# Two token tiles per weight unit in three products, and three small moves in a two-block transformer kernel

## The chip, the cores and the metric

The kernel runs on one core of one Trainium2 chip. Its time is the device time of one execution, in microseconds; the time given for a kernel is the median of its runs. The engines are TensorE (PE, with its weight loads shown apart as PEld), VectorE (DVE), ScalarE (ACT), GpSimd (POOL) and SyncE (SP, which here only starts transfers). Each runs its own program in order, and they meet through semaphores.

## The reference

Two transformer blocks on 512 tokens of width 1024, in float32, the second one also on 256 context tokens.

```python
# first block
h = rmsnorm(x, g_pre); proj = h @ w_in         # split into qa ka va gate_a qi ki wi qb kb vb fb gate_b
att_a = dsa_branch(...)                        # top-k chosen keys, softmax
att_b = fox_branch(...)                        # causal attention with a decay
y_a = (att_a * silu(gate_a)) @ w_branch_a;  y_b = (att_b * silu(gate_b)) @ w_branch_b
m_a, m_b = split(sigmoid(h @ w_merge))
out = (m_a * y_a + m_b * y_b) @ w_out          # chunks wo0, wo1
x = x + rmsnorm(out, g_post)                   # x1
e = p @ w_ple                                  # chunks ple0, ple1
gate = sigmoid(x @ w_ple_gate)                 # chunks pg0, pg1
x = x + rmsnorm(gate * e, g_ple)               # x2
# second block, layer 0 (even) and layer 1 (odd)
hx = rms_norm(x, norm_pre) * (1 + sc_x) + sh_x; px = hx @ w_in   # the same for the context
mx = even_mixer(...)   # differential attention (two score maps) over context and own keys, short convolution
x = x + g_x * rms_norm(mx @ w_out, norm_post)  # chunks eo0, eo1; the result is x3
mx = odd_mixer(...)    # neighbourhood attention, Fourier mixing
x = x + g_x * rms_norm(mx @ w_out, norm_post)  # chunks oo0, oo1
```

## The kernel before

Every large product is made in three passes: each float32 operand is split into a rounded high part and the rest, its low part, and high·high, high·low and low·high are added up in PSUM. The weights come as one stream of **granules** of 1 MB, each of four **units** (128 rows by 512 columns), into the two halves of a buffer `RAW` (L1415, SP). For each unit ACT copies the high part to its place (`high`, L1439), and POOL subtracts it from the raw weights for the low part (`low_weights`, L1258). SP loads a granule once the one before the last has been split. PE waits for both parts of a unit (`w_hi`, `w_lo`). Most units go round a ring of four places (`ROOM`); for some chunks spare places are free, so that eight or more units can lie ready: the first four of wo1 and of oo1, all of eo1.

A product of 512 tokens is either computed **unit by unit** (`gemm`: for each unit, all four token tiles of 128, in four PSUM banks) or **tile by tile** (`by_tiles`, L784 to L812, and the loop at L1234 to L1244 for oo1): all eight units for the first token tile, then all eight for the second, and so on. The first tile waits for each unit as it is made; the other three find them there. Tile by tile, a tile's result is complete before the next begins, and the engines behind it can start on it. The order of PE's program is written out by hand; the other engines' programs follow it by hand too.

**Around wo1.** PE runs wo0 (unit by unit), wo1 (L967, tile by tile), ple0 and ple1. For each tile t of wo1 DVE copies the result out of PSUM (L2436), multiplies by g_post (L2132), inverts the root (L2138) and adds to x (L2143), in this order and tile after tile. ACT squares and sums the tile after DVE's copy (`norm_tile`, L1476), then takes the root (L1478). ACT makes the high weights of ple0 after the root of tile 2 (L1726), and those of ple1 after tile 3; POOL makes the low ones behind that.

**Around x2.** pg1 is computed tile by tile. For each tile t ACT runs one step of a loop (L1765 to L1773):

```python
gate_out(4 + t)                    # sigmoid of pg1's tile t, from PSUM
if t: x2_squared(t - 1)            # waits for DVE's x2, then square (L1476) and root (L1478)
high(UNITS["e_q"][min(3 * t + 1, 7)] if t < 3 else UNITS["e_k"][3])
act.wait_ge(sig("ge"), 5 + t)      # DVE has multiplied the gate and e
norm_tile("e", t, M_E[t], 4)       # square and root of e
```

Sigmoid and square root need different function tables on ACT; a load of one is an ACT_TABLE_LOAD in the trace. It stands where the program first needs the other function. Square and copy need no load in either state. After the last step ACT squares x2's tile 3; DVE normalises (L2489), and PE turns the normalised tiles (L819), which it needs before e_q of the 512 tokens. Meanwhile PE computes e_q and e_k for the context from the weights that ACT's loop makes.

**The even attention** has 48 steps: per pair of heads four short ones (context queries, scores 128 by 256) and eight wide ones (128 by 768). `score_even` (L1032) puts the two score maps of a step m = 0, 1 at bank 2m; a wide map takes that bank and the next (`open_two`). DVE takes the maxima (L2550), ACT the exponentials (L1829), which free the banks; between the scores PE works on slices of other products.

**Around eo1.** eo0 (unit by unit), eo1 (L1129, tile by tile, after tile 0 the turning of a modulation row, L757), then both for the context, then the turning of x3 (L819). Per tile, ACT copies the result (L1930), stores x3 of the tile before and squares it, squares this tile, and DVE weighs, inverts and adds; then the next tile. ACT makes n_q's weights after the last tile's squares. x3n, written by DVE at L2647, is what the turning waits for.

**Around oo1**, the last product: ACT squares each tile from PSUM (L2097), DVE multiplies and adds to x3, SP and ACT store it.

**The start.** SP loads x in four transfers, then granules 0 and 1, then constants. ACT squares and roots the four tiles of x, makes unit 0's high part, and takes x turned by PE out of PSUM; DVE makes its low part (L2177). `keys` is the first product.

## Time and profile before

| | us |
|---|---|
| median of 3 runs (lowest, highest) | 1278.9 (1278.81, 1279.24) |
| the profiled execution, and its span from first to last instruction | 1282.1, 1280.3 |
| PE busy in the span | 1235.3 (96%) |
| DVE busy | 673.2 (53%) |
| ACT busy | 632.9 (49%) |
| POOL busy | 461.6 (36%) |

All times in the text are counted from the start of the span. Matmuls are pipelined: the record of a 512-column matmul is 0.39 us long, but the next one starts 0.23 us after it, so "busy" for PE covers small losses, and an idle time in brackets counts only from the end of the record before. `[1.62 <-POOL w_low L1258]` behind an instruction says that the engine was idle for 1.62 us ahead of it and that POOL's instruction of line 1258 released it. In rows by windows, PEclk is the TensorE clock granted, as a share of 2.4 GHz: 0.50 is 1.2 GHz.

### The profile page before, as it was taken

The page shows a single profiled execution, that of the slowest core. Times are in us where ns is not written, and L with a number is a line of the kernel's source. Part 1 is how long each engine was busy: PE and PEld are TensorE (multiplying, and loading weights), DVE is VectorE, ACT ScalarE, POOL GpSimd, SP SyncE. Part 2 cuts the span into 40 slices and gives each one's busy share as a digit, 9 for nine tenths or more (in the row PEclk, how much of TensorE's full clock was granted, in tenths as well). Part 3 has the DMA queues.
Part 4 walks back from the last instruction along what each step waited for, and adds up shares of the span by engine and source line. Part 5 has one row for each costly group of instructions (what it writes and reads, how often), then busy time and mean ns, then how long its engine had stood idle before and what let it go on. Part 6 is the DMA issues. An engine that isn't in the chain of part 4 may idle for free. (4 is left out here: it accounts for less than half of the span.)

```text
span 1280.3 us, 19570 instructions
## 1 busy us (share of the span) xinstructions
PE 1235.3 (96%) x7148; PEld 990.4 (77%) x7148; DVE 673.2 (53%) x1294; ACT 632.9 (49%) x1354; POOL 461.6 (36%) x360
## 2 busy tenths in 40 slices
PE   7999999999999999899999999999999999999997
PEld 5877777776788788788878888787878788777785
DVE  4576965755314254647475765723815600655453
ACT  6544327655533356723366666626345422645433
POOL 5544343321344535612332333332343123322351
PEclk9999999999999999999999999999999999999999
DMA  6332541111322613230434322211254221222542
GB/s 234 117 98 70 194 165 66 45 47 36 133 94 94 225 72 132 75 140 25 153 113 190 130 83 100 100 67 52 89 215 145 90 103 66 100 67 67 175 134 87
DMA packets 28429, 140.33 MB, mean 110 GB/s; under 512 B 4304, under 2 KB 5712, under 8 KB 15728
## 3 DMA queue, kind: packets, MB, share of 16 engines
q1 hardware_dynamic: 21584, 117.72, 26.0%
q10 hardware_dynamic: 6752, 21.35, 5.0%
q8 instruction: 60, 0.98, 0.3%
q14 instruction: 33, 0.27, 0.1%
HBM read 122.74 MB, written 6.29 MB: 101 GB/s over the span
## 5 line engine op out<-in xcount | busy, mean ns | idle before, releaser
L1258 POOL TENSOR_TENSOR w_low<-w_raw,w_high 128x512 fp32r<-128x512 f32 x256 | 348.7, 1375 | 641.7 <-ACT w_high L1439 641.1
L1439 ACT CAST w_high<-w_raw 128x512 fp32r<-128x512 f32 x256 | 153.8, 622 | 259.3 <-PE psum L663 170.6
L663 PE MATMUL psum<-x_high,w_high 128*128 128x512 f32 x528 | 219.2, 415 | 4.6 <-DVE x_low L2177 1.0
L663 PE MATMUL psum<-x_high,w_low 128*128 128x512 f32 x528 | 206.6, 391 | 0.0
L663 PE MATMUL psum<-x_low,w_high 128*128 128x512 f32 x528 | 206.2, 391 | 0.0
L663 PEld LDWEIGHTS psum<-x_high,w_high 128*128 128x128 f32 x528 | 99.6, 189 | 34.1 <-issue 10.1
L663 PEld LDWEIGHTS psum<-x_high,w_low 128*128 128x128 f32 x528 | 99.1, 188 | 21.6
L663 PEld LDWEIGHTS psum<-x_low,w_high 128*128 128x128 f32 x528 | 99.6, 189 | 16.6 <-issue 1.0
L663 PE MATMUL psum<-w_high,x_high 128*128 128x512 f32 x224 | 88.3, 394 | 0.8 <-POOL w_low L1258 0.6
L2550 DVE TENSOR_REDUCE small<-psum 128x1 f32<-128x768 f32 (+1 forms) x96 | 70.0, 771 | 35.3 <-PE psum L1043 35.3
L663 PE MATMUL psum<-w_high,x_low 128*128 128x512 f32 x224 | 87.3, 390 | 0.0
L663 PE MATMUL psum<-w_low,x_high 128*128 128x512 f32 x224 | 87.2, 389 | 0.0
L1287 POOL TENSOR_SCALAR arena<-arena,small 128x768 f32<-128x768 f32 (+1 forms) x48 | 40.5, 844 | 96.6 <-DVE small L2557 96.6
L1829 ACT ACTIVATE arena<-psum,small 128x768 f32<-128x768 f32 (+1 forms) x84 | 63.3, 760 | 14.3 <-DVE small L2550 13.9
L1838 ACT COPY arena<-psum 128x512 f32<-128x512 f32 (+1 forms) x80 | 36.7, 459 | 66.5 <-PE psum L1051 66.1
L663 PEld LDWEIGHTS psum<-w_high,x_high 128*128 128x128 f32 x224 | 42.0, 188 | 14.2 <-issue 4.5
L663 PEld LDWEIGHTS psum<-w_high,x_low 128*128 128x128 f32 x224 | 42.1, 188 | 8.9
L663 PEld LDWEIGHTS psum<-w_low,x_high 128*128 128x128 f32 x224 | 42.1, 188 | 8.4
L691 PE MATMUL psum<-x_high,w_high 128*128 128x512 f32 x96 | 42.1, 438 | 0.5 <-DVE arena L2543 0.5
L2562 DVE SCALAR_TENSOR_TENSOR arena<-arena,small 128x768 f32<-128x768 f32 (+1 forms) x36 | 30.1, 835 | 19.5 <-POOL arena L1287 19.5
L691 PE MATMUL psum<-x_high,w_low 128*128 128x512 f32 x96 | 37.8, 394 | 0.0
L691 PE MATMUL psum<-x_low,w_high 128*128 128x512 f32 x96 | 37.6, 392 | 0.0
(484 smaller groups left out, 2807.0 us busy)
## 6 DMA issues: line engine op xcount, KB each, us to landing
w_raw<-stream SPq DMA_DIRECT2D x98, 1024.0 KB, 4.9
x_kept<-arena ACTq DMA_DIRECT2D x8, 512.0 KB, 4.6
arena<-x_kept ACTq DMA_DIRECT2D x8, 512.0 KB, 5.6
arena<-bias ACTq DMA_DIRECT2D x8, 512.0 KB, 4.5
q_masked<-e_q_high SPq DMA_DIRECT2D x24, 96.0 KB, 2.5
arena<-x SPq DMA_DIRECT2D x4, 512.0 KB, 5.2
arena<-x ACTq DMA_DIRECT2D x4, 512.0 KB, 5.1
arena<-ctx ACTq DMA_DIRECT2D x4, 512.0 KB, 4.5
```

The lines of the kernel that those rows point to most:

```text
L663: mm = pe.matmul(o, l, r, start=(first and n == 0 and kind != "fc"), stop=(last and n == len(passes) - 1))
L691: mm = pe.matmul(o, l, r, start=k == 0 and n == 0, stop=k == NK - 1 and n == 2)
L1258: pool.tensor_tensor(PLACE[u][1], RAW[:, g % 2, u % 4, :], PLACE[u][0].bitcast(F32), ALU.subtract).then_inc(w_lo, 1)
L1287: pool.tensor_scalar(second, second, SM[:, RINV + c + 1:RINV + c + 2], SM[:, 82:83], ALU.mult, ALU.mult)\
L1439: act.copy(PLACE[u][0], RAW[:, g % 2, u % 4, :]).then_inc(w_hi, 1)
L1829: frees(act.activation(map_place(s, m), PS[:, 512 * b:512 * b + w], ACT.Exp, bias=scr(NEGMAX + c), accum_out=scr(ROWSUM + c)), key)
L1838: frees(act.copy(E_PT[:, 2 * (d % 2) + hh, P * c:P * c + w], ps[:, 0:w]), key)
L2550: dve.tensor_reduce(scr(NEGMAX + 2 * (s % 4) + m), PS[:, 512 * b:512 * b + w], AX.X, ALU.max, negate=True).then_inc(sig("e_neg"), 1)
L2562: dve.scalar_tensor_tensor(e0, e0, scr(RINV + c), e1, ALU.mult, ALU.add).then_inc(sig("e_p"), 1)
```

## The change

1. `by_tiles` gets a parameter `together`: the first `together` token tiles are computed side by side, unit by unit, in as many banks, and the rest tile by tile. wo1 and eo1 use `together=2`. oo1's own loop is replaced by `by_tiles` with `together=2`; its last tile now takes the units in the order 4 to 7, 0 to 3, as the other chunks did.
2. In ACT's loop round x2, a square root of a single column stands right after each sigmoid.
3. In the even attention, short steps use banks 2m and 2m + 1 in turn.
4. Granule 0 comes in two transfers: unit 0 alone, with its own semaphore (`stored`, which counts 16 more at the end for it), and units 1 to 3.

```diff
--- before.py
+++ after.py
@@ -781,35 +781,37 @@
                 if chunk in GUEST and GUEST[chunk][1] < 4:
                     due.append(GUEST[chunk])
 
-            def by_tiles(chunk, x, after=None, gives_back=True):
+            def by_tiles(chunk, x, after=None, gives_back=True, together=1):
 
                 units = UNITS[chunk]
-                for t in range(ST):
-                    rows = slice(P * t, P * t + P)
-                    acc = next_bank((chunk, t))
-                    ks = [*range(4, NK), *range(4)] if t == ST - 1 else range(NK)
+                for first in [0, *range(together, ST)]:
+                    group = range(together) if first == 0 else (first,)
+                    accs = {t: next_bank((chunk, t)) for t in group}
+                    ks = [*range(4, NK), *range(4)] if ST - 1 in group else range(NK)
                     for k in ks:
                         u = units[k]
-                        if t == 0:
+                        if first == 0:
                             pe.wait_ge(w_hi, u + 1)
                             pe.wait_ge(w_lo, u + 1)
                             unit_read.add(u)
                         (hi, lo), (wh, wl) = x[k], PLACE[u]
-                        for n, (l, w) in enumerate(((hi, wh), (hi, wl), (lo, wh))):
-                            mm = pe.matmul(acc[:, :], l[:, rows], w, start=k == ks[0] and n == 0,
-                                           stop=k == ks[-1] and n == 2)
-                        if k == ks[-1]:
-                            fills_bank(mm, (chunk, t))
-                            bk, n = fills[chunk, t]
-                            done = (bank_full[bk], n + 1)
-                        elif t == ST - 1 and gives_back:
-                            used[0] += 1
-                            mm.then_inc(w_used, 1)
-                            done = (w_used, used[0])
-                        if t == ST - 1 and gives_back:
-                            unit_done[u] = done
+                        for t in group:
+                            rows = slice(P * t, P * t + P)
+                            for n, (l, w) in enumerate(((hi, wh), (hi, wl), (lo, wh))):
+                                mm = pe.matmul(accs[t][:, :], l[:, rows], w, start=k == ks[0] and n == 0,
+                                               stop=k == ks[-1] and n == 2)
+                            if k == ks[-1]:
+                                fills_bank(mm, (chunk, t))
+                                bk, n = fills[chunk, t]
+                                done = (bank_full[bk], n + 1)
+                            elif t == ST - 1 and gives_back:
+                                used[0] += 1
+                                mm.then_inc(w_used, 1)
+                                done = (w_used, used[0])
+                            if t == ST - 1 and gives_back:
+                                unit_done[u] = done
                     if after:
-                        after(t)
+                        after(first)
 
             def turns(name, tiles, src, ks):
 
@@ -964,7 +966,7 @@
             gemm("wo0", X, ready=split("mrg_lo"))
 
 
-            by_tiles("wo1", X)
+            by_tiles("wo1", X, together=2)
             gemm("ple0", B, ready=turned("pT"))
             gemm("ple1", B)
 
@@ -1036,7 +1038,7 @@
                     pe.wait_ge(sig(f"{kind}_stacked{hh}"), 96 * (pr + 1))
                 for m in range(2):
                     key = ("e", "S", s, m)
-                    acc = (open_two if x else open_bank)(key, 2 * m)
+                    acc = open_two(key, 2 * m) if x else open_bank(key, 2 * m + s % 2)
                     q, k = stack("q", head, m)[0:96, c:c + P], stack("k", head, m)[0:96]
                     for c0 in range(0, w, 512):
                         c1 = min(c0 + 512, w)
@@ -1126,7 +1128,7 @@
             pool[0] = (3, 7, 4, 5, 6)
             gemm("eo0", mixed, mixed_c, ready=lambda k: pe.wait_ge(sig("mix_lo"), 3 * (k // 2) + 3), part="x")
             pool[0] = (0, 1, 2, 6, 4)
-            by_tiles("eo1", mixed, lambda t: turn_due(), gives_back=False)
+            by_tiles("eo1", mixed, lambda t: turn_due(), gives_back=False, together=2)
             pool[0] = (3, 7)
             for k in range(NK):
                 unit("eo0", k, mixed, mixed_c, "c")
@@ -1231,17 +1233,7 @@
                            ("fmix", j))
             mixed = [(KH[:, k, 0:S], KL[:, k, 0:S]) for k in range(4)] + X[4:]
             gemm("oo0", mixed, ready=split("nix_lo"))
-            for t in range(ST):
-                rows = slice(P * t, P * t + P)
-                acc = next_bank(("oo1", t))
-                for k, u in enumerate(UNITS["oo1"]):
-                    if t == 0:
-                        pe.wait_ge(w_hi, u + 1)
-                        pe.wait_ge(w_lo, u + 1)
-                    (hi, lo), (wh, wl) = mixed[k], PLACE[u]
-                    for n, (l, w) in enumerate(((hi, wh), (hi, wl), (lo, wh))):
-                        mm = pe.matmul(acc[:, :], l[:, rows], w, start=k == 0 and n == 0, stop=k == NK - 1 and n == 2)
-                fills_bank(mm, ("oo1", t))
+            by_tiles("oo1", mixed, gives_back=False, together=2)
 
 
         SSQ, NEGMAX, ROWSUM, RINV, TOP8 = 0, 16, 24, 32, 40
@@ -1252,7 +1244,9 @@
             def low_weights(first, last):
                 for u in range(first, last + 1):
                     g = granule_of(u)
-                    if u % 4 == 0:
+                    if u == 0:
+                        pool.wait_ge(sig("stored"), 16)
+                    elif u % 4 == 0 or u == 1:
                         pool.wait_ge(raw_in[g % 2], 16 * (g // 2 + 1))
                     pool.wait_ge(w_hi, u + 1)
                     pool.tensor_tensor(PLACE[u][1], RAW[:, g % 2, u % 4, :],
@@ -1412,6 +1406,11 @@
                         filled(sp, ("mod%d_%d" % mod, 0))
                     else:
                         sp.wait_ge(sig("mod_half"), MODS.index(mod) + 1)
+                if g == 0:
+                    sp.dma_start(RAW[:, 0, 0, :], dram["stream"][0][:, 0:512]).then_inc(sig("stored"), 16)
+                    sp.dma_start(RAW[:, 0, 1:4, :].rearrange("p a n -> p (a n)"),
+                                 dram["stream"][0][:, 512:]).then_inc(raw_in[0], 16)
+                    continue
                 sp.dma_start(RAW[:, g % 2, :, :].rearrange("p a n -> p (a n)"),
                              dram["stream"][g]).then_inc(raw_in[g % 2], 16)
             for t in range(ST):
@@ -1432,7 +1431,9 @@
                 while at[0] <= min(upto, N_UNITS - 1):
                     u = at[0]
                     g = granule_of(u)
-                    if u % 4 == 0:
+                    if u == 0:
+                        act.wait_ge(sig("stored"), 16)
+                    elif u % 4 == 0 or u == 1:
                         act.wait_ge(raw_in[g % 2], 16 * (g // 2 + 1))
                     if before_in_place[u] is not None:
                         act.wait_ge(*unit_done[before_in_place[u]])
@@ -1766,6 +1767,7 @@
                 if t == 3:
                     high(UNITS["e_k"][0])
                 gate_out(4 + t)
+                act.activation(scr(95), scr(95), ACT.Sqrt)
                 if t:
                     x2_squared(t - 1)
                 high(UNITS["e_q"][min(3 * t + 1, 7)] if t < 3 else UNITS["e_k"][3])
@@ -2099,7 +2101,7 @@
                 act.activation(scr(8 + t), scr(8 + t), ACT.Sqrt, bias=scr(SSQ + t), scale=1.0 / D).then_inc(sig("out_root"), 1)
             act.wait_ge(sig("x4"), 2 * ST)
             act.dma_start(columns_of(out, ST - 1)[:, :, 512:], N_O[:, ST - 1, 512:]).then_inc(sig("stored"), 16)
-            act.wait_ge(sig("stored"), 2 * 16 * ST)
+            act.wait_ge(sig("stored"), 16 + 2 * 16 * ST)
 
 
         @block.vector
```

## Rows read from the trace of the kernel before

**Rows 1.** The granted clock over the whole span.

```profile
core 0: 1280.3 us, clock 0.995
```

**Rows 2.** PE's waits: waiting line, releaser; us in total, times, longest us.

```profile
PE psum L1043 <- ACT arena L1829: 2.9, 2, 1.5
...
PE psum L799 <- POOL w_low L1258: 2.5, 4, 1.6
PE psum L651 <- POOL w_low L1258: 2.5, 2, 2.1
PE psum L819 <- DVE merge_a L2489: 2.2, 1, 2.2
...
PE psum L1243 <- ACT w_high L1439: 1.5, 1, 1.5
```

**Rows 3.** Timeline of PE, wo1 and the start of ple0: start us, us, what.

```profile
436.12 0.39 PE L799 MATMUL psum<-k_high,x_high 128*128 128x512 f32 x1
...
440.61 0.47 PE L799 MATMUL psum<-w_high,x_high 128*128 128x512 f32 x1 [1.62 <-POOL w_low L1258]
...
444.34 0.47 PE L799 MATMUL psum<-w_high,x_high 128*128 128x512 f32 x1 [0.30 <-POOL w_low L1258]
...
461.44 0.39 PE L663 MATMUL psum<-w_high,b_high 128*128 128x512 f32 x1
```

**Rows 4.** Timeline of the other engines round wo1.

```profile
439.20 5.00 POOL L1258 TENSOR_TENSOR w_low<-w_raw,w_high 128x512 fp32r<-128x512 f32 x4 [5.81 <-ACT w_high L1439]
445.37 0.69 DVE L2436 COPY arena<-psum 128x512 f32<-128x512 f32 x1 [19.40 <-PE psum L799]
...
450.75 0.69 DVE L2436 COPY arena<-psum 128x512 f32<-128x512 f32 x1 [0.32 <-PE psum L799]
...
456.20 0.69 DVE L2436 COPY arena<-psum 128x512 f32<-128x512 f32 x1 [0.76 <-PE psum L799]
...
459.12 1.50 POOL L1258 TENSOR_TENSOR w_low<-w_raw,w_high 128x512 fp32r<-128x512 f32 x1 [14.92 <-ACT w_high L1439]
```

**Rows 5.** By windows: stretch, its us, busy time of each engine, PEclk, DMA.

```profile
437.81:441.22 3.41, 1.79 (x9) 1.13 (x7) 0.00 (x0) 2.79 (x6) 2.02 (x2) 1.00 0.92 387
...
547.06:550.47 3.41, 3.41 (x18) 3.41 (x17) 1.89 (x4) 1.14 (x2) 1.09 (x1) 0.50 1.06 401
```

**Rows 6.** Timeline of ACT, DVE and PE round x2.

```profile
510.79 1.28 ACT L1478 ACT_TABLE_LOAD   x1
510.88 2.13 DVE L2132 TENSOR_TENSOR merge_a<-merge_a,arena 128x1024 f32<-128x1024 f32 x1 [1.35 <-ACT q_masked L1476]
...
523.94 1.06 ACT L1476 ACTIVATE q_masked<-arena 128x1024 fp32r<-128x1024 f32 x1 [1.89 <-DVE arena L2143]
...
525.11 1.28 ACT L1478 ACT_TABLE_LOAD   x1
...
545.84 2.56 PE L819 MATMUL psum<-squares_sb,merge_a 128*128 128x128 f32 x16 [2.25 <-DVE merge_a L2489]
```

**Rows 7.** Timeline of PE and DVE round eo1.

```profile
943.60 0.39 PE L799 MATMUL psum<-q_masked,b_high 128*128 128x512 f32 x1
...
952.11 0.95 PE L757 MATMUL psum<-sel_sb,mod_rows 128*128 128x2 f32 x8
...
979.03 0.75 DVE L2647 TENSOR_SCALAR merge_a<-arena,small 128x1024 f32<-128x1024 f32 x1
...
985.69 0.27 PE L819 MATMUL psum<-squares_sb,merge_a 128*128 128x128 f32 x1
```

**Rows 8.** Timeline of PE and ACT, oo1.

```profile
1248.41 0.39 PE L1243 MATMUL psum<-x_high,k_high 128*128 128x512 f32 x1
...
1273.79 0.60 ACT L2097 ACTIVATE q_masked<-psum 128x512 fp32r<-128x512 f32 x1 [4.42 <-PE psum L1243]
```

**Rows 9.** Timeline of PE, the first matmul of the first product.

```profile
13.95 0.47 PE L663 MATMUL psum<-x_high,w_high 128*128 128x512 f32 x1 [0.97 <-DVE x_low L2177]
```

**Rows 10.** Timeline of PE, the scores of the second short step.

```profile
636.18 0.47 PE L1043 MATMUL psum<-b_both,q_masked 96*128 96x256 f32 x2
```

## The prediction, written before the change was run

> **What bounds the kernel now.** I read the busy times first: TensorE (PE) is busy 96% of the span (in the table of the profile), at a mean granted clock of 0.995 [rows 1], so a change gives time only where it removes PE waiting or keeps PE's clock up. Next, PE's waits with their releasers [rows 2]: the product loop of L799 waits 2.5 us for GpSimd's (POOL's) low weights in wo1, the last product (L1243) 1.5 us for the high weights, the turning of x2 (L819) 2.2 us for the normalised x2, the even scores (L1043) 2.9 us for ScalarE's (ACT's) exponentials. Then the timeline round each edited place, and the granted clock in windows. The records overlap (0.39 us each), so a loss is read from starts: after the last stall of wo1, 75 matmuls start in 461.44 − 444.34 = 17.10 us [rows 3], 0.228 each; I use 0.227, as the first of them is slower. One unit of one token tile is 3 matmuls, 0.68 us; POOL makes a unit's low half in 5.00 / 4 = 1.25 us [rows 4]. A tile that runs while its weights are being made is therefore paced by POOL, and two tiles per unit (1.36 us) are not.
>
> **Paired tiles, product by product.** At full pace 96 matmuls take 21.8 us.
>
> wo1: PE spends 461.44 − 436.12 = 25.3 us [rows 3], 3.5 above pace. Paired, unit 4 is read at 436.12 + 4 × 1.36 = 441.6 and was there at 440.6 [rows 3]; later units come each 1.25 us and are read each 1.36. So no wait is left inside wo1, and it ends at 457.9. But ple0 follows it, and ple0's weights are not ordered by PE: ACT makes them after the squares of wo1's third tile, and each tile's squares wait for VectorE's (DVE's) copy of that tile, which stands behind the whole chain of the tile before (copy, weigh, reciprocal, add). From the DVE rows: tile 0's chain ran 445.37 to 450.43 (the next copy started at 450.75 after 0.32 idle), 5.06 us with a table load in it; tile 1's ran 450.75 to 455.44, 4.69 [rows 4]. Now tile 0 is full 1.2 us later: its last matmul is the 45th of the pair, at 436.12 + 44 × 0.227 = 446.1, against 444.34 + 2 × 0.227 = 444.8. Its copy starts at 446.6, tile 1's at 451.7, tile 2's at 456.4, against 456.20 [rows 4]. POOL then ends ple0's first unit 0.2 us after its present 459.12 + 1.50 = 460.6 [rows 4], and PE starts ple0 at 460.95 instead of 461.44. Of 3.5 us removed 0.5 remains; 2.9 us become one wait of PE before ple0.
>
> That wait has a second price. After PE had been idle 2.25 us before 545.84 [rows 6], the clock row that follows is at 0.50, that is 1.2 GHz for 3.41 us [rows 5]; the 1.62 us idle before 440.61 [rows 3], with PE busy 1.79 of 3.41 us, was in a stretch that was followed by no such fall. A 2.9 us idle lies above both, so I take a fall: 3.41 / 2 = 1.7 us, as ple0 and ple1 are dense. wo1 in sum: −0.5 + 1.7 = +1.2 us; ends −1.0 (the DVE chain shorter where POOL is quiet) and +2.0 (PE starts ple0 0.3 later than now, and the fall). The Trainium skill (TensorE: Matmul & The Clock Gate, Part 1) agrees that idle time brings the lower level, and says the monitor runs freely, so the place of a fall can differ from run to run; no row of one profile shows the latter.
>
> eo1: tile 0 runs 943.60 to 952.11 [rows 7], 8.5 us against 24 × 0.227 = 5.4: 3.1 us lost. Paired, its last unit is read at 943.60 + 7 × 1.36 = 953.1, later than PE had it now. The turned row of the modulation moves behind tile 1; it is late by 2.4 us, still before DVE's first weighing. The tiles' chain on ACT and DVE starts 1.8 us later, but tile 1's then starts only when tile 0's is through, where now it waited for PE; I get 0.4 us later at its end. It ends at 979.03 + 0.75 = 979.8 now, so 980.2; PE, 3.1 earlier, needs it at 985.69 − 3.1 = 982.6 [rows 7]. Cover 2.4 us, so all 3.1 is kept: −3.1, ends −3.3 and −2.0 (half of the cover's slip eaten by the weights of n_q, which ACT makes behind the same chain).
>
> oo1: PE starts at 1248.41 and ACT reads its last tile at 1273.79 [rows 8]. At pace the last matmul starts at 1248.41 + 95 × 0.227 = 1270.0 and ACT reads it 0.5 us after (as 444.8 to 445.37 at wo1 [rows 3, 4]): 1270.45, so −3.3. Unit 4 is read at 1253.85. Its weights, the slowest thing here, are there by 1252.77, when PE left its 1.5 us wait for them [rows 2]. Behind oo1 stand only a square, a root and the store of each tile. Tiles 0 and 1 arrive together at 1259 and are long through when tile 3 comes. Ends −3.5 and −2.5.
>
> A second bank is opened ahead of each pair. The banks it takes were last used one product earlier and emptied before this product's inputs existed; cost 0.
>
> **Root table behind the sigmoid.** In each of four steps ACT makes a sigmoid, squares x2 of the step before, roots, makes weights, squares e, roots. In the third step the square at 523.94 comes after 1.89 us of idle and the load of the root table follows at 525.11 for 1.28 us [rows 6]. Loaded in that idle time (1.28 + 0.2 for the tiny root, 1.48 < 1.89), it saves 1.3 us; the fourth step is built alike, and I take 1.1 for it, as the gain of the third has moved its square up already. The first step pays: there the load (510.79) now runs beside DVE's weighing (510.88 to 513.01) [rows 6]; moved, it stands before the square that this weighing waits for, so square and weighing come 1.5 us later and the root 0.2 later. Through weighing and add, x2 of tile 0 is 1.5 later, which the second step sees less its 1.3 us of waiting for its own table: +0.5. Sum 0.5 − 1.3 − 1.1 = −1.9 at the last x2, for which PE waits at 545.84 [rows 6]; the weights of e_k, made in the same steps, move with it. Its own shift of about 2 us leaves the wait before 545.84 as long as it is, and so the fall of the clock behind it. Ends −2.6 (first step free) and +0.5 (third and fourth step gain nothing).
> By the Trainium skill (ScalarE: Activation LUTs, What ACT_TABLE_LOAD costs) a switch is 1.28 us of load and about 1.38 of drain. The rows have the load and no drain: the load begins at 525.11, as the square's record ends. By the page's figure the first step would pay 2.8 and the edit bring about −0.5.
>
> **Short even scores in alternating banks.** At the second short step PE starts its scores at 636.18 with no idle noted [rows 10]: the bank was free already. PE's 2.9 us of waits at L1043 [rows 2] are of the 96x512 form, the wide steps, whose banks don't change. Cost 0. Nothing queued moves: the order on PE is the same. Ends −0.5 and +1.7 (one more fall of the clock).
>
> **First unit's own transfer.** The first product starts at 13.95 waiting for DVE's x_low [rows 9], not for weights. ACT, which waited for the transfer, would begin 0.6 us earlier and then wait for PE's transposes as now. SP issues one transfer more ahead of the constants; they are needed ten us later. Cost 0, ends −0.3 and +0.5.
>
> **Sum.** +1.2 − 1.9 − 3.1 − 3.3 = −7.1 us. The profiled execution took 1282.1 (span 1280.3, 1.8 around it) and becomes 1275.0; it stands 3.2 above the median of 1278.9, from which the same 7.1 gives **1271.8 us**.
>
> **Rivals.** (a) The wait before ple0 brings no fall of the clock, as the one before 440.61 brought none: −7.1 − 1.7 = −8.8, 1270.1. (b) The three pairings give their whole 3.5 + 3.1 + 3.3, if ACT had ple0's weights in time: with the table −11.8, 1267.1. For it: it takes only that the third tile's squares come 3 us earlier. Against it: DVE's chain of 4.7 us a tile leaves no such 3 us. (c) The chain eats more: eo1's cover of 2.4 us is used up and the table gains nothing because the first step's delay is carried through: +1.2 + 0 − 2.0 − 3.0 = −3.8, 1275.1. For it: four engines' steps interlock there, and DVE's records are 2.13 instead of 1.23 where POOL works beside it. (d) Slower: PE's clock. A mean clock of 0.995 is 0.005 × 1280.3 = 6.4 us lost, under four falls [rows 1], while waits of 2.1 (L651) and 1.6 us (L799) [rows 2, 3] are there that could each bring one once everything has shifted. A fall costs up to 1.7; six more give 1278.9 − 7.1 + 10.2 = 1282.0, slower, and from the fifth on the gain is gone. Against it: the three runs lie within 0.4 us, which a moving set of falls would spread. (e) The change doesn't do what it says: PE waits at each pair for its second bank. Then only the table is left, 1277.0; the order of banks speaks against it.
>
> **Numbers.** Forecast 0.50, (a) 0.24, (b) 0.04, (c) 0.13, (d) 0.04, (e) 0.05. A measurement here can tell 0.2% (2.6 us) from no change: faster is below 1276.3, which is the forecast, (a), (b) and (c) nearly whole: 0.88; same 0.09; slower 0.03. All ends added give 1267.7 to 1276.6 about; with the corners cut, 1268.7 to 1275.8 leaves out less than 2 in 10.
>
> **What would show it.** Right: no wait at the paired loops except, in wo1's place, one of 2.5 to 3.2 us before the first matmul of ple0, with a clock row of 0.50 behind it; ple0 starting within 0.6 us of its old distance from wo1's start (25.3 us); eo1 first to last matmul 3 us shorter and no new wait at the turning of x3; PE from oo1's first matmul to ACT's last read 22.0 us; the square of x2 in the third step followed by a root with no load between. Wrong: ple0 starting 22 us after wo1 (then ACT's order did not hold it), a wait for a bank before a pair, or the turning of x2 no earlier against the start of pg1.

## The result, and the profile after

| | before | changed |
|---|---|---|
| median of 4 runs each, same chip (lowest to highest), us | 1279.07 (1278.81 to 1279.77) | 1272.42 (1270.49 to 1274.71) |
| the profiled execution, and its span | 1282.1, 1280.3 | 1270.49, 1268.6 |
| PE busy in the span | 1235.3 | 1229.3 |

The ratio of the medians is 0.9941, 95% interval 0.9924 to 0.9957: faster by 6.65 us. The forecast was 1271.8. One run of experiment e5, its profiled one, took 2441.48 us and one of e7 1367.35 us, so both are left out of the medians below, and the trace of e9, the same kernel as e5, is read in place of e5's.

The granted clock of the changed kernel (before: [rows 1]):

```profile
core 0: 1268.6 us, clock 0.997
```

PE's waits: waiting line, releaser; us in total, times, longest.

```profile
PE psum L663 <- POOL w_low L1252: 4.0, 3, 2.7
...
PE psum L1045 <- ACT arena L1831: 2.7, 2, 1.4
...
PE psum L821 <- DVE merge_a L2491: 2.3, 1, 2.3
PE psum L651 <- POOL w_low L1252: 1.3, 2, 0.9
```

Against [rows 2], the waits of the paired loops (L801 now) are gone, and so is oo1's for the high weights. In their place L663 has one wait of 2.7 us: ple0's. The wait for x2 (L821) is as long as it was; the longest of those for e_k's weights (L651), which ACT makes in the same steps as the early roots, fell from 2.1 to 0.9 us.

To compare two traces I measure PE's stretches between the same matmuls of its program (start to start); what lies between two neighbouring rows differs by 0.14 us or less, and an F marks a stretch with a fall of the clock to 0.50 in it.

| stretch of PE | before | changed | difference | forecast |
|---|---|---|---|---|
| start of the span to the first product | 13.95 | 14.78 | +0.83 | 0 |
| wo1 to ple0 | 25.32 | 24.67 | −0.65 | −0.5 |
| ple0 to ple1 | 5.44 | 5.54 | +0.10 | +1.7 (a fall) |
| e_q for the context to the turning of x2 | 24.07 | 21.53 | −2.54 | −1.9 |
| behind it, to the first matmul of e_q for the tokens | 9.11 F | 7.55 | −1.56 | 0 |
| even scores 0 to 9 | 32.29 | 32.04 | −0.25 | 0 |
| even scores 9 to 10 | 6.96 F | 5.55 | −1.41 | 0 |
| even scores 33 to 34 | 7.15 F | 7.12 F | −0.03 | 0 |
| eo1, its first 24 matmuls (before: tile 0; now: units 0 to 3 of tiles 0 and 1) | 8.51 | 5.44 | −3.07 | −3.1 |
| six matmuls in the odd attention, from 1118.11 (1109.54 now) to the next of L1206 (L1208 now) | 1.84 | 2.12 | +0.28 | 0 |
| oo1, first to last matmul | 24.95 | 21.53 | −3.42 | −3.3 |
| all, to the last matmul (1273.37, 1261.62) | | | −11.75 | |

Three kinds of numbers stand in this table. −0.65, −2.54, −3.07 and −3.42, −9.7 together, are the change. −1.56 and −1.41 are falls of the clock which the profiled run of before had and this one had not. +0.83 is the clock once more, at the start: PE turns x at 1.2 GHz until the chip first grants 2.4, at 11.2 us in the one profile and 12.9 in the other. The +0.28 is none of the change: the place takes 1.84 us in e6, whose code there is the changed kernel's, too. The two profiled runs, 11.6 us apart, thus overstate the change by some 2 us, and the medians show less than the 9.7.

The one fall ahead of the last matmul in the changed kernel's profile, behind the even scores 33 (timeline, and the window that begins with the fall):

```profile
762.47 0.59 PE L1045 MATMUL psum<-k_high 96*128 96x512 f32 x2 [1.37 <-ACT arena L1831]
```

```profile
763.81:767.22 3.41, 3.41 (x29) 2.75 (x27) 3.37 (x5) 1.80 (x4) 3.26 (x3) 0.50 0.02 5
```

**Round ple0**, ACT, DVE, POOL and PE of the changed kernel (start us, us; against [rows 3, 4]):

```profile
456.85 0.68 DVE L2438 COPY arena<-psum 128x512 f32<-128x512 f32 x1
...
457.62 1.06 ACT L1477 ACTIVATE q_masked<-arena 128x1024 fp32r<-128x1024 f32 x1 [3.12 <-DVE arena L2438]
...
459.01 1.12 ACT L1440 CAST w_high<-w_raw 128x512 fp32r<-128x512 f32 x2
459.75 3.70 POOL L1252 TENSOR_TENSOR w_low<-w_raw,w_high 128x512 fp32r<-128x512 f32 x2 [16.23 <-ACT w_high L1440]
...
461.48 0.47 PE L663 MATMUL psum<-w_high,b_high 128*128 128x512 f32 x1 [2.75 <-POOL w_low L1252]
```

This is the chain the prediction drew: DVE copies the third tile, ACT squares it and only then makes ple0's high weights, POOL the low ones, and PE has been waiting for 2.75 us. Wo1 itself lost nothing any more; 24.67 − 21.8 = 2.9 is this wait (the bracket counts only from the end of the last record).

**Round x2**, ACT's third step, DVE's first weighing and PE (against [rows 6]):

```profile
512.27 2.10 DVE L2134 TENSOR_TENSOR merge_a<-merge_a,arena 128x1024 f32<-128x1024 f32 x1 [2.87 <-ACT q_masked L1477]
...
517.00 0.29 ACT L1479 ACTIVATE small<-small,cols_sb 128x1 f32<-128x1 f32 x1
...
522.15 1.28 ACT L1770 ACT_TABLE_LOAD   x1
523.45 0.20 ACT L1770 ACTIVATE small<-small 128x1 f32<-128x1 f32 x1
524.03 1.06 ACT L1477 ACTIVATE q_masked<-arena 128x1024 fp32r<-128x1024 f32 x1 [0.38 <-DVE arena L2145]
525.00 0.18 ACT L1477 ACTIVATION_READ_ACCUMULATOR q_masked<-arena 128x1 f32 x1
525.22 0.30 ACT L1479 ACTIVATE small<-small,cols_sb 128x1 f32<-128x1 f32 x1
...
543.45 1.97 PE L821 MATMUL psum<-squares_sb,merge_a 128*128 128x128 f32 x16 [2.25 <-DVE merge_a L2491]
```

The load stands where 1.5 of the 1.89 idle microseconds were, and the root of the third step follows its square without one.

**Round eo1 and oo1**, PE, DVE and ACT (against [rows 7, 8]):

```profile
938.09 0.62 PE L801 MATMUL psum<-q_masked,b_high 128*128 128x512 f32 x2
...
973.81 0.76 DVE L2649 TENSOR_SCALAR merge_a<-arena,small 128x1024 f32<-128x1024 f32 x1
...
977.12 0.27 PE L821 MATMUL psum<-squares_sb,merge_a 128*128 128x128 f32 x1
...
1240.09 0.39 PE L801 MATMUL psum<-x_high,k_high 128*128 128x512 f32 x1
...
1262.04 0.60 ACT L2099 ACTIVATE q_masked<-psum 128x512 fp32r<-128x512 f32 x1 [4.42 <-PE psum L801]
```

DVE ends 977.12 − 974.57 = 2.55 us before the turning of x3 needs it, and PE comes to that turning with no idle; from oo1's start ACT reads the last tile after 21.95 us, where it took 25.38.

### The profile page after: what moved, and what is told of

Read it like the earlier page. It is cut to its first block, busy times and chain, and to the rows that moved or that the text cites. A ratio compares the mean times of both kernels' runs of the same rounds, so it can differ in the third digit from the quotient of the medians.

```text
span 1268.6 us, 19585 instructions
## 1 busy us (share of the span) xinstructions
PE 1229.3 (97%) x7148; PEld 989.0 (78%) x7148; DVE 673.9 (53%) x1294; ACT 631.7 (50%) x1358; POOL 462.2 (36%) x360
## 4 chain that ended last, share of the span: by engine, by line
PE 78%; DVE 10%; ACT 7%; issue 2%; DMA 1%; POOL 1%; DVEq 0%; ACTq 0%; POOLq 0%; SPq 0%
PE psum L663 47%; PE psum L691 6%; PE psum L801 4%; PE psum L843 2%; PE psum L1069 2%; DVE arena L2342 2%; DVE small L2339 2%; PE psum L938 2%; PE psum L1045 2%; PE psum L1053 2%; PE psum L651 2%; PE psum L921 1%; POOL w_low L1252 1%; PE psum L1208 1%; PE psum L1176 1%
## 5 line engine op out<-in xcount | busy, mean ns | idle before, releaser
L663 PE MATMUL psum<-x_high,w_high 128*128 128x512 f32 x528 | 219.2, 415 | 4.6 <-DVE x_low L2179 1.0
L663 PE MATMUL psum<-x_high,w_low 128*128 128x512 f32 x528 | 206.5, 391 | 0.0
L663 PE MATMUL psum<-x_low,w_high 128*128 128x512 f32 x528 | 206.3, 391 | 0.0
L663 PEld LDWEIGHTS psum<-x_high,w_high 128*128 128x128 f32 x528 | 99.6, 189 | 34.1 <-issue 10.1
L663 PEld LDWEIGHTS psum<-x_high,w_low 128*128 128x128 f32 x528 | 99.1, 188 | 21.6
L663 PEld LDWEIGHTS psum<-x_low,w_high 128*128 128x128 f32 x528 | 99.6, 189 | 16.6 <-issue 1.0
L663 PE MATMUL psum<-w_high,x_high 128*128 128x512 f32 x224 | 88.4, 395 | 0.8 <-POOL w_low L1252 0.6
L663 PE MATMUL psum<-w_high,x_low 128*128 128x512 f32 x224 | 87.3, 390 | 0.0
L663 PE MATMUL psum<-w_low,x_high 128*128 128x512 f32 x224 | 87.2, 389 | 0.0
L663 PEld LDWEIGHTS psum<-w_high,x_high 128*128 128x128 f32 x224 | 42.0, 188 | 14.2 <-issue 4.5
L663 PEld LDWEIGHTS psum<-w_high,x_low 128*128 128x128 f32 x224 | 42.0, 188 | 8.9
L663 PEld LDWEIGHTS psum<-w_low,x_high 128*128 128x128 f32 x224 | 42.1, 188 | 8.4
```

What stands on the lines that cost most here:

```text
L663: mm = pe.matmul(o, l, r, start=(first and n == 0 and kind != "fc"), stop=(last and n == len(passes) - 1))
```

## The experiments

Each kernel is the changed one with the edit shown, if nothing else is said. Medians are us; "before" was 1279.69 on the chip of e1 to e4, 1279.38 for e5 to e8, 1279.68 for e9 to e11. A profile shows one run, so the edits are judged by PE's stretches, and the medians stand beside them.

**e1: ple0's weights before the second squaring.** Is ACT's order alone what makes PE wait before ple0?

```
-                if t == 2:
-                    high(UNITS["ple0"][1])
+                if t in (1, 2):
+                    high(UNITS[f"ple{t - 1}"][1])
```

> The changed kernel with one edit: ACT makes ple0's high weights after the root of wo1's tile 1 (not tile 2) and ple1's after the root of tile 2 (not tile 3). Theory A (ACT's order holds ple0 back): the 2.7 us of idle before ple0's first matmul goes; ple0 starts 21.8 us after wo1 instead of 24.7, and the turning of x1 comes 2.9 us nearer to wo1's start. Nothing waits at ple1. With no long idle time there, no fall of the clock there either: median 2.9 to 4 us below the changed kernel's 1272.4, so about 1269. Rival B (DVE's chain of four tiles sets x1, and only the place of the wait moves): ple0 starts early, but the turning of x1 waits for x1 and keeps at most 1 us; median 1271.5 to 1272.5.

Median 1271.51 (1269.41 to 1274.22), ratio 0.9937 (0.9924 to 0.9949). Wo1 to ple0 took 21.76 us, with no wait: 2.9 less. But from the turning of x1 to pg1 it took 30.75 instead of 27.06. ACT and PE, and the clock of the stretch behind:

```profile
469.43 1.14 ACT L1440 CAST w_high<-w_raw 128x512 fp32r<-128x512 f32 x2 [1.67 <-DVE arena L2145]
470.48 2.04 ACT L1736 COPY merge_a<-psum 128x512 f32<-128x512 f32 x4
472.38 2.08 ACT L1739 CAST x_high<-psum 128x512 fp32r<-128x512 f32 x4
473.85 0.80 PE L663 MATMUL psum<-w_high,x_high 128*128 128x512 f32 x1 [2.09 <-DVE x_low L2164]
```

```profile
473.55:476.96 3.41, 3.11 (x7) 2.49 (x8) 2.04 (x4) 0.91 (x2) 0.00 (x0) 0.50 0.00 0
```

PE now reached pg0 earlier, but ACT's copies of ple1 stood behind its wait for x1 (1.67 us idle), and the turned x1 behind them. The wait moved from ple0 to pg0, and the clock fell there. So the median is the one of rival B and not the 1269 of theory A, but the wait stands where neither put it: before pg0 and its x_low, not before the turning of x1.

**e5 and e9: e1's edit, and ACT's wait for x1 (with the context's transfers) moved behind its copies of ple1.** Both are one kernel. e1's lines are not shown again.

```
             for c in range(2):
-                if c:
-                    act.wait_ge(sig("x1"), ST)
-                    ...                         # the context's transfers
                 ahead(f"ple{c}")
                 ...                             # the copies of ple{c}
+                if c:
+                    act.wait_ge(sig("x1"), ST)
+                    ...
```

> The edit of e1_early (ACT makes ple0's and ple1's high weights one tile earlier), and ACT waits for x1 and loads the context rows after its copies of ple1 instead of before. In e1_early PE started ple0 2.9 us earlier, but ple1's copies stood behind the wait for x1, so XH came late and pg0's first matmul waited 2.1 us for x_low. Theory A, mended: with the copies out of the way ACT can take the turned x1 at once. From wo1's first matmul to pg1's first 59.8 us (62.6 in the changed kernel, 63.4 in e1_early), no wait over 0.6 us in between and so no fall of the clock there. Median 1269 to 1270. Rival B (x1 itself, made tile after tile by DVE, is what PE meets): x1T waits for DVE and the stretch stays above 61.5 us.

> The changed kernel, with ACT's copies of wo1 ordered ahead as before and, in addition, ple0's first split hoisted ahead of ACT's second squaring as well, and ACT's wait for x1 and its context transfers put behind its copies of ple1. Theory A (the 2.7 us in front of ple0 is only the splits of ple0 standing behind ACT's and DVE's norm work, and the extra late x_low at pg0 came from ACT's wait for x1): from wo1 to ple0 21.8 us instead of 24.7, and from ple0 to pg1 38.0 as in the changed kernel, so the chain ends 2.9 us earlier; with two falls of the clock 1269.5 (range 1268.5 to 1271). Rival B (the transfer of the context, issued later, is late for its norm): from the first e_q unit to the turning of x2, or before it, 1 to 3 us come back, and the total is 1271 to 1273.

Medians 1269.65 (ratio 0.9923, 0.9909 to 0.9936) and 1269.57 (0.9918, 0.9905 to 0.9932). e9's PE:

```profile
457.33 0.39 PE L663 MATMUL psum<-w_high,b_high 128*128 128x512 f32 x1
...
470.86 0.50 PE L663 MATMUL psum<-w_high,x_high 128*128 128x512 f32 x1 [0.73 <-DVE x_low L2164]
```

Ple0 starts 21.76 us after wo1, the wait at pg0 is 0.73 instead of 2.09, and that stretch is 27.59 long, 0.5 over the changed kernel's. The stretch up to the turning of x2 is 21.87, 0.3 longer (21.67 in e11, whose code is the same up to there). So 2.9 − 0.5 − 0.3 = 2.1 us are kept. Theory A of e9's expectation holds but for these 0.8; the rival asked for 1 to 3 to come back.

**e2: wo1 tile by tile again, eo1 and oo1 paired.**

```
-            by_tiles("wo1", X, together=2)
+            by_tiles("wo1", X)
```

> The changed kernel with wo1 tile by tile again. Theory A: ple0 starts 25.3 us after wo1 instead of 24.7, so 0.6 us are lost at most, and PE's 2.7 us before ple0 is spread over four waits of 1.6, 0.3, 0.3, 0.3 us, which brought no fall of the clock in the kernel before. Median between 0.6 above and 1 below the changed kernel (1271.5 to 1273.0): the same. Rival C (pairing wo1 is worth its full 3.5 us): 1275.5 to 1276.

Median 1272.18 (1268.4 to 1274.63), ratio 0.9935. The old wait at unit 4 is back and the one before ple0 gone:

```profile
440.32 0.47 PE L801 MATMUL psum<-w_high,x_high 128*128 128x512 f32 x1 [1.52 <-POOL w_low L1252]
...
461.14 0.39 PE L663 MATMUL psum<-w_high,b_high 128*128 128x512 f32 x1
```

Wo1 to ple0 took 25.23 us: pairing wo1 is worth 0.56 us, of the 3.5 that it removes inside the product. No median shows it: this one lies 0.2 below the changed kernel's.

**e3: no early root. e6: an early root from the third step on.**

```
-                act.activation(scr(95), scr(95), ACT.Sqrt)      # e3 only this
+                if t > 1:                                       # e6
+                    act.activation(scr(95), scr(95), ACT.Sqrt)
```

> The changed kernel without the single-column root behind the sigmoid. Theory: from pg1's first matmul to the turning of x2 46.5 us as in the kernel before, instead of 43.9; the root of x2's tile 2 has its table load behind the square again. 2.5 us more: 1274.9. Rival (the gain at x2 comes from somewhere else, and the load costs nothing or is hidden anyway): 43.9 us stay, and the median stays near 1272.4.

> The changed kernel with the single-column root only in the third and fourth step of the loop round x2. I had forecast that the root in the first step costs 0.5 us further on; the changed kernel's trace had the root of x2's tile 0 at the same place as before (517.00 against 516.90 with the stretch 0.14 later), and the third and fourth step 1.3 us earlier each. Theory: from e_q's first matmul of the context to the turning of x2 21.6 us, as in the changed kernel: the first two steps' roots neither pay nor cost. Rival (the first step pays and something else gave more): 21.1 us or less.

e3: median 1272.46 (1272.23 to 1274.78), ratio 0.9944; e_q for the context to the turning of x2 23.90 us, as before the change, with ACT's third step as it was:

```profile
523.65 1.06 ACT L1477 ACTIVATE q_masked<-arena 128x1024 fp32r<-128x1024 f32 x1 [1.91 <-DVE arena L2144]
524.62 0.19 ACT L1477 ACTIVATION_READ_ACCUMULATOR q_masked<-arena 128x1 f32 x1
524.82 1.28 ACT L1479 ACT_TABLE_LOAD   x1
```

A fall at 537.9 lies inside that stretch, but it eats into the wait for x2 (1.4 us here) and not into its end, which hangs on ACT's steps. The stretch without the early root and without a fall in it is 24.07 before the change and 24.05 in e8. The root is thus worth 2.4 to 2.5 us in the stretch. The median forecast for e3, 1274.9, did not come: 1272.46 is the changed kernel's, as the rival said of it, so the stretches show the root's worth and the medians do not. e6: median 1270.76 (1270.3 to 1272.94), ratio 0.9937 (0.9922 to 0.9952); that stretch 21.49, so the early root in the first two steps neither gives nor costs anything. In e6 the first step's load stands behind its square again:

```profile
510.84 1.28 ACT L1479 ACT_TABLE_LOAD   x1
```

**e4: the even banks and the first unit's transfer undone.**

```
-                    acc = open_two(key, 2 * m) if x else open_bank(key, 2 * m + s % 2)
+                    acc = (open_two if x else open_bank)(key, 2 * m)
```

(and granule 0 in one transfer, waited for as before)

> The changed kernel with two parts undone: short even scores all in banks 0 and 2, and granule 0 in one transfer. Theory: both are worth nothing. The first product's first matmul and the even steps stand at the same distances; PE's start of the first product at 13.9 or up to 0.9 later by the level of the clock during the turning of x (it was at half until 12.9 us in the changed kernel's profile, until 11.2 in the other). Median within 0.6 of 1272.4. Rival (the first unit's transfer is worth the 0.6 us that ACT waited; alternating banks let the scores go ahead): 0.6 to 2 us more.

Median 1271.56 (1269.69 to 1271.87), ratio 0.993: nothing lost. Even scores 0 to 9 took 32.25 instead of 32.04, so the banks give about 0.2 (the three profiles with the old banks have 32.14 to 32.29, the others 32.03 to 32.06). The first product starts at 14.35, inside the 13.56 to 15.02 of the kernels with the transfer, so that is worth nothing that can be seen. This profile also has what the changed kernel's has not, a fall right behind the wait before ple0:

```profile
461.06 0.47 PE L663 MATMUL psum<-w_high,b_high 128*128 128x512 f32 x1 [2.75 <-POOL w_low L1250]
...
462.60 0.63 PE L663 MATMUL psum<-w_high,b_high 128*128 128x512 f32 x1
463.03 0.63 PE L663 MATMUL psum<-w_low,b_high 128*128 128x512 f32 x1
```

```profile
462.40:465.81 3.41, 3.41 (x10) 2.63 (x9) 2.00 (x4) 2.83 (x6) 1.80 (x2) 0.50 0.00 0
```

Matmuls start 0.43 us apart at 0.50 against 0.23, and ple0 took 7.14 us instead of 5.54: a fall costs 1.6 us. The instructions there and the idle of 2.75 us are the changed kernel's.

**e8: before, with only eo1 and oo1 paired.**

```
+            by_tiles("eo1", mixed, lambda t: turn_due(), gives_back=False, together=2)
+            by_tiles("oo1", mixed, gives_back=False, together=2)
```

> The kernel before with nothing but the pairing of eo1 and of oo1. Theory: eo1's first tile is 3.07 us shorter and oo1 3.42, as in the changed kernel, and all stretches between are as before: 6.5 us below the kernel before, whose median on that chip is 1279 to 1280, so 1273. By this the rest of the change (wo1, table, banks, first transfer) brings 3 us free of the clock's falls and little in the median. Rival (the pairings need the earlier edits, or the tiles' chains of ACT and DVE take part of it back): 4 us or less.

Median 1271.88 (1269.86 to 1273.8), ratio 0.9941 (0.9929 to 0.9954). Eo1's stretch is 5.44, oo1's 21.53, as in the changed kernel: 6.5 us. Up to the even phase its work is that of before, so it shows whether the fall behind the turning of x2 [rows 5, 6] belongs to the code:

```profile
546.14 1.97 PE L821 MATMUL psum<-squares_sb,merge_a 128*128 128x128 f32 x16 [2.25 <-DVE merge_a L2481]
```

```profile
547.40:550.80 3.40, 3.40 (x31) 3.40 (x30) 1.78 (x4) 1.14 (x2) 1.07 (x1) 1.00 1.06 401
```

It does not: the same wait, 2.25 us to the digit, and the clock stays at 1.00. The median is 0.5 below that of the whole change and 1.1 below the 1273 expected. So what wo1 and the root bring, 3.2 us by the stretches, stands in no difference of medians; with four and five runs some 4 us apart they cannot decide it.

**e7 and e10: useless matmuls where PE idles.** e7 has 11 before ple0 and 9 before the turning of x2; e10 has also 6 each before the even scores 9 and 33. Nothing of the output depends on them.

```
+                for _ in range(n):
+                    pe.matmul(BANK[b][:, :], X[0][0][:, 0:P], X[0][0], start=True, stop=True)
```

> The changed kernel with matmuls of no use (results overwritten) on PE where it was idle: 11 before ple0 (2.5 us) and 9 before the turning of x2 (2.0 us). Theory D (a fall of the clock follows a stretch in which PE idles): nothing starts later, ple0 stays 24.7 us after wo1 and the turning of x2 21.6 us after e_q's first, and neither stretch is followed by a fall in any run, so that the runs' median is about 1 us lower (one of the other kernel's profiles had the fall behind ple0, two had it behind x2's turning) and their spread smaller. Rival (the falls come at random times or from load, not from idling): falls stay as frequent, median as in the changed kernel or higher.

> The changed kernel with useless matmuls (128x512, 0.216 us each) in TensorE's four idle places: 11 before ple0, 9 before the turning of x2, 6 each before the even scores 9 and 33; nothing of the output depends on them. Theory A (every fall of the granted clock in these traces follows an idle of 1.4 to 2.7 us of TensorE, and the scatter of 3 to 4 us between runs is whether a fall follows each of the idles): no stretch of 0.5 between the first product and the last matmul, the profiled run 1.6 us per lost fall under the changed kernel's, the median 1268.8 (range 1268 to 1270), all runs within 1.5 us of each other. Rival B (the falls are placed by something else than the idle): stretches of 0.5 stay at about 663 and 764, the median 1271 to 1272.5, scatter of 3 us.

e7: median 1270.5 (1268.84 to 1272.14), ratio 0.993; no fall at the two filled places, falls at 662.4 and 764.8, the two left open. e10: median 1270.05 (1268.44 to 1272.29), ratio 0.9925 (0.9913 to 0.9938), clock 0.999, and no fall between the first product and the last matmul:

```profile
459.04 2.43 PE L821 MATMUL psum<-x_high 128*128 128x512 f32 x10
...
461.75 0.47 PE L663 MATMUL psum<-w_high,b_high 128*128 128x512 f32 x1 [0.28 <-POOL w_low L1268]
...
661.71 0.47 PE L1059 MATMUL psum<-b_both,q_masked 96*128 96x512 f32 x1
```

```profile
457.00:460.40 3.40, 3.40 (x17) 2.81 (x15) 2.05 (x4) 2.48 (x5) 0.40 (x1) 1.00 0.00 0
661.00:664.40 3.40, 3.31 (x30) 2.33 (x30) 3.29 (x6) 3.13 (x8) 1.20 (x1) 1.00 0.00 0
```

The even scores 33 to 34, 7.12 to 7.18 us in the profiles with a fall there, take 5.53. But half of theory A's expectation failed: the median lies just outside its range of 1268 to 1270 and the runs 3.9 us apart, not 1.5, and two of the five have a clock of 0.997, so falls presumably came in them still, at places that no trace shows. The filler also cost 0.3 us before the turning of x2; why scores 10 to 33 took 96.25 us here, with 95.78 in the changed kernel and 95.90 in e11, I did not find out.

**e11: e9 with the fillers of the even phase, the best.**

```
+                if s in (9, 33):
+                    busy_at(6, 5)
```

> The kernel of the early split and the later wait for x1, with 6 useless matmuls of 128x512 before each of the even scores 9 and 33. Theory A (idle brings the fall): against the same kernel without them two falls less, 1.5 us each where both had fallen: 1267.0 (range 1266 to 1268.5). Rival B (falls have another cause): as without them, 1269.5; and if the useless matmuls are late work on TensorE themselves, 0.3 to 0.6 us more.

Median 1268.19 (1265.41 to 1268.67), ratio 0.9904 (0.9889 to 0.9919). That is inside the range of theory A. Its four runs lie below 1268.7; e9's median is 1269.57, with an interval that overlaps, so the 1.4 us between them are likely and not shown. Its even phase had no fall, scores 9 to 10 in 5.55 and 33 to 34 in 5.53 us; its profiled run fell once, behind the turning of x2 (541.9), which costs 1.6.

## Why the prediction came out right, step by step

**Wo1, −0.5: right (−0.65, and −0.56 by e2).** The mechanism, that POOL's pace inside the product only hides a chain on DVE and ACT behind it, is shown by e1: with ACT's order changed, ple0 starts 2.9 us earlier. Rival (b), all pairings whole, had the condition that ACT makes ple0's weights in time: e1 and e9 supply it, and e9 keeps 2.1 of the 2.9. What the prediction held against (b), that DVE's chain of 4.7 us a tile leaves no such 3 us, was wrong: that chain sets the squares, but only the order of ACT's program puts ple0's weights behind them.

**The fall behind it, +1.7: right in size, wrong as a certainty.** e4 has it (1.6 us), the changed kernel's profile not, with the same idle. Forecast and rival (a) are the same kernel in two kinds of runs. This shows in the times: the changed kernel's runs of 1270.49, 1271.32, 1273.52 and 1274.71 us had a mean clock of 0.997, 0.996, 0.995 and 0.993. It is not all of the scatter: two runs of e8 with the same 0.998 took 1269.86 and 1273.31, two of e11 1265.41 and 1268.67. The start of the first product moves by up to 1.5 us outside that mean; the rest is open. The prediction's last argument against rival (d), that three runs within 0.4 us exclude a moving set of falls, failed: 33 runs of the kernel before on these chips lie between 1277.83 and 1281.93. Three alike were luck.

**The early root, −1.9: right in kind, but the term of the first step was mis-sized.** It was priced at +0.5, though the prediction's own terms, 1.5 later less 1.3 saved, give +0.2, and it is 0 (e6 against the changed kernel: 21.49 and 21.53). The weighing of the first step does come later, 512.27 instead of 510.88 + 0.14 (the 0.14 is how much later this profile is there), 1.25 us against 1.5 forecast. But the second step's root, at 517.00, is where it was (516.90 + 0.14), because that step no longer waits for its own load: the delay carried over and the load saved cancel whole. The third and fourth step gave 2.5, forecast 2.4. Of the load itself, the Trainium skill (ScalarE: Activation LUTs, What ACT_TABLE_LOAD costs) adds 1.38 us of drain to 1.28 of load; here the load starts at 522.15, as the sigmoid's record ends, and the next operation starts at 523.45, 0.02 behind the load. No row shows a drain, and the −0.5 worked out from that figure does not hold: the edit brought 2.4 to 2.5.

**The wait for x2 stays, and its fall with it: the wait yes (2.25 us before and after), the fall by the run.** Before, e1, e2 and e11 have a fall within 2 us of that turning, e3 one 8 us ahead of it; the changed kernel, e4, e6, e8 and e9 none. The Trainium skill (TensorE: Matmul & The Clock Gate, Part 1) says that the monitor behind the clock runs freely and does not start anew with a kernel; that the same wait has a fall behind it in before and none in e8, equal in their work up to there, agrees with it.

**Eo1, −3.1: right (−3.07).** The chain on ACT and DVE ended 0.3 us later against eo1's start (36.48 us behind it, 36.18 before), forecast 0.4, and the cover left was 2.55, forecast 2.4. **Oo1, −3.3: right (−3.42).** e8 shows both alone, without the other edits.

**Banks and first transfer, 0 and 0: right within 0.25 us** (e4).

**The sum.** Forecast for no fall −8.8; the four terms measured give −9.7. Over the 33 runs of before (median 1279.53) and the eight of the changed kernel and e6, whose stretches are equal (1271.05), the difference is 8.5. So the missing 1.2 us are the falls that the new wait before ple0 sometimes adds, or others; one in four profiles that have that wait and no filler (changed, e3, e4, e6) shows one, which explains 0.4. The rest is open. That the forecast of 1271.8 lies 0.6 from the median owes something to luck, two errors against each other: a fall counted as certain, and an early root counted 0.6 too low. One more sum of the prediction is wrong: its upper ends add up to 1279.1 and not to 1276.6, so the stated range of 1268.7 to 1275.8 cut off more at the top than it said.

## What to carry to other kernels

When a loop is slowed by a producer, look at who stands behind the loop before pricing the cure: a product made 3.5 us shorter started its successor only 0.6 us earlier, since the successor's weights stood behind another chain in ACT's program. One hoisted instruction group plus one wait moved down (e9) then let out 2.1 us more. Neither is worth this alone: before the change PE came to ple0 without idling [rows 3], so the earlier weights would have had nothing to shorten there (they were not run without the pairing). Cover decides the rest: the same pairing was worth its full 3.1 and 3.4 us where the next reader came 2.5 us after its data, or where nothing followed. And compare traces by stretches between equal instructions, with the clock's falls taken out: runs of one kernel lie 2 to 6 us apart here, and medians of four or five runs could not rank kernels that differ by 3 us in their stretches.

## What the runs showed of the hardware

The place of the clock's falls is not a property of the program. A fall inside these profiles cost 1.4 to 1.6 us. All twenty between first product and last matmul, in the twelve profiles read, began inside an idle time of PE of 1.4 to 2.8 us or within 2.2 us of its end. But the same idle brought one in some runs and none in others: where nothing filled it, 1 of 4 profiles with the wait of 2.75 us before ple0 had a fall, 4 of 9 with the 2.25 us before the turning of x2, 6 of 10 and 7 of 10 with the 1.3 to 1.5 us before the even scores 9 and 33. Matmuls in the idle kept the clock up at all eight filled places in the profiles of e7, e10 and e11, and cost 0 to 0.3 us each. The start of the first product, 13.56 to 15.02 us, goes with the moment at which full clock is first granted (10.4 to 13.0 us), which no edit here moved on purpose.
